# Moving the large SBUF tiles of a three-layer kernel to multiples of 512 bytes

## The reference, cut to what matters

```python
def swiglu(x, w_gate, w_up, w_down):
    return (jax.nn.silu(x @ w_gate) * (x @ w_up)) @ w_down
...
        x = layer_norm(DN_ALPHA * x + y, mix_ln_g[layer], mix_ln_b[layer])
        x = layer_norm(DN_ALPHA * x + swiglu(x, ffn_w_gate[layer], ffn_w_up[layer], ffn_w_down[layer]),
                       ffn_ln_g[layer], ffn_ln_b[layer])
...
    ff = jnp.square(jax.nn.relu(h2 @ w_ff1 + b_ff1)) @ w_ff2 + b_ff2
```

## Time and profile before

| | |
|---|---|
| three runs | 3600.16, 3602.02, 3602.89 us; median 3602.02 us |
| profiled execution, first to last instruction | 3599.7 us |
| around it, against the median | 2.3 us |
| PE busy | 3523.2 us, 98%, 16054 matmuls |
| VectorE, ScalarE, GpSimd busy | 50%, 34%, 15% |
| DMA queue of the loads | 22.5% of 16 engines' span |
| mean granted TensorE clock | 0.987 |

### The profile page before, as it was taken

How to read it: one execution, slowest core, us unless ns; L and a number is a source line. 1 busy time by engine, 2 the same in 40 slices (tenths; PEclk the granted TensorE clock), 3 DMA queues, 4 the chain that set the end, 5 groups by cost and what they waited for, 6 DMA issues and landing times. The chain is left out here.

```text
span 3599.7 us, 41711 instructions
## 1 busy us (share of the span) xinstructions
PE 3523.2 (98%) x16054; PEld 2827.2 (79%) x16054; DVE 1782.8 (50%) x2319; ACT 1234.6 (34%) x1795; POOL 529.2 (15%) x302
## 2 busy tenths in 40 slices
PE   9999999999999999999999999999999899999998
PEld 7768888888887777767888888888877778888886
DVE  7986423233256666667423233564567774323235
ACT  4444410111144444455311112355454442212133
POOL 0007100000042000013100000253223530000004
PEclk9999999999999999999999999999999999999999
DMA  3102213122122111112213123322231222111113
GB/s 105 40 30 89 94 60 109 47 78 86 47 82 82 48 41 47 41 59 77 88 59 105 52 84 108 93 89 94 97 99 48 76 88 88 53 45 48 47 58 100
DMA packets 77474, 259.12 MB, mean 72 GB/s; under 512 B 10288, under 2 KB 11696, under 8 KB 77360
## 3 DMA queue, kind: packets, MB, share of 16 engines
q1 hardware_dynamic: 77360, 257.59, 22.5%
HBM read 244.45 MB, written 4.72 MB: 69 GB/s over the span
## 5 line engine op out<-in xcount | busy, mean ns | idle before, releaser
L202 PE MATMUL ps<-xh,whi 128*128 128x512 f32 x2712 | 941.8, 393 | 14.2 <-POOL xl L494 8.9
L202 PE MATMUL ps<-xh,wlo 128*128 128x512 f32 x2712 | 934.4, 390 | 0.0
L202 PE MATMUL ps<-xl,whi 128*128 128x512 f32 x2712 | 934.1, 390 | 0.0
L185 DVE TENSOR_TENSOR wlo<-stage,whi 128x1024 fp32r<-128x1024 f32 (+1 forms) x361 | 507.2, 1405 | 477.9 <-ACT whi L178 476.7
L178 ACT ACTIVATE whi<-stage 128x1024 fp32r<-128x1024 f32 (+1 forms) x361 | 377.8, 1046 | 1001.2 <-PE ps L202 973.8
L202 PEld LDWEIGHTS ps<-xh,whi 128*128 128x128 f32 x2712 | 511.1, 189 | 130.0 <-POOL xl L494 9.1
L202 PEld LDWEIGHTS ps<-xh,wlo 128*128 128x128 f32 x2712 | 511.2, 188 | 107.3
L202 PEld LDWEIGHTS ps<-xl,whi 128*128 128x128 f32 x2712 | 511.5, 189 | 105.1
L202 PE MATMUL ps<-hh,whi 128*128 128x512 f32 x1216 | 421.5, 395 | 3.1 <-DVE hl L2938 1.6
L202 PE MATMUL ps<-hl,whi 128*128 128x512 f32 x1216 | 420.3, 394 | 0.0
L202 PE MATMUL ps<-hh,wlo 128*128 128x512 f32 x1216 | 420.3, 394 | 0.0
(11 more groups left out here) (453 smaller groups left out, 4013.1 us busy)
## 6 DMA issues: line engine op xcount, KB each, us to landing
stage<-in_w_ff SPq DMA_DIRECT2D x88, 512.0 KB, 3.5
stage<-in_w_gate SPq DMA_DIRECT2D x59, 512.0 KB, 3.4
stage<-in_w_up SPq DMA_DIRECT2D x59, 512.0 KB, 3.4
stage<-in_w_in SPq DMA_DIRECT2D x50, 512.0 KB, 3.4
ada<-in_w_ada SPq DMA_DIRECT2D x48, 512.0 KB, 3.5
stage<-in_w_qkv SPq DMA_DIRECT2D x43, 512.0 KB, 3.4
stage<-in_w_down SPq DMA_DIRECT2D x48, 448.0 KB, 3.3
stage<-in_w_out SPq DMA_DIRECT2D x24, 512.0 KB, 3.4
```

The lines of the kernel that those rows point to most:

```text
L185: dve.tensor_tensor(wlo[slot][:, n], stage[slot][:, n], whi[slot][:, n].bitcast(F32), ALU.subtract).then_inc(w_split, 1)
L202: done = pe.matmul(acc[:, h * HALF:(h + 1) * HALF], wt[slot][:, w], xt[:, b, h * HALF:(h + 1) * HALF], start=b == 0 and wt is whi and xt i ...
```

## The change

It moves tiles, and changes no instruction but for the addresses in it. On all five engines the instructions stand in the same order, with the same shapes and waits.

```diff
+    LINE = 512
+
+    def to_line(name):
+        at = -(-nc.sbuf_base // 32) * 32
+        if at % LINE:
+            sb(name, [P, (LINE - at % LINE) // 4])
+        return nc.sbuf_base
+
+    mod = sb("mod", [P, NMOD, DB])
+    moments = sb("moments", [P, 2, 24])
+    to_line("pad_x")
     x = sb("x", [P, DB, S])
     XH_AT = nc.sbuf_base
     xh = sb("xh", [P, DB, S], F32R)
...
-    mv = sb("mv", [P, 2, 2])
     stats = sb("stats", [P, 2, 2, 6])
-    sd = sb("sd", [P, 2, 1])
-    rstd = sb("rstd", [P, 2, 1])
...
-    mod = sb("mod", [P, NMOD, DB])
     gb2 = sb("gb2", [P, DB])
...
-    moments = sb("moments", [P, 2, 24])
...
-    REGION = -(-nc.sbuf_base // 32) * 32
+    REGION = to_line("pad_region")
```

## The result

| | before | after |
|---|---|---|
| median | 3602.45 us (4 runs, 3600.16 to 3604.06) | 3582.72 us (4 runs, 3581.69 to 3584.48) |
| ratio | | 0.9949, 95% interval 0.9937 to 0.9962 |
| profiled span | 3599.7 us | 3580.5 us |

By the medians the kernel is 19.7 us faster, 0.55%; the ratio, which is not the quotient of the two medians, says 0.51%, and its interval reads as 13.7 to 22.7 us. The forecast was 3578 us, 24.1 us less than before.

The account below looks back on a forecast made before the run. TensorE, busy 98% of the span with a stream of matmuls, was taken as the bound. The profiled 3599.7 us less 24.1 gave 3575.6, plus 2.3 for the median, so 3578 us; range 3485 to 3606 us.

Parts of the forecast that it names:

- the side that had 0.77: Whole kernel: chance of any faster outcome, 0.60 for the region-only forecast plus 0.17 for everything getting faster.
- Matmuls on `hh` go from 233.2 to 226.6 ns: Down projections: with region and fixed tiles at 0, their matmuls reach the up projections' rate of 226.6 ns.
- 3648 matmuls x 6.6 ns: Down projections: 3 x 1216 matmuls at 233.2 - 226.6 ns less each, 24.1 us, all on the path.
- The fixed tiles at 0 bring nothing: Matmuls on `xh`, `xl`: moving fixed tiles from 128 to 0 taken as zero; bounds 96 us gain, 124 us loss.
- The count of 9360: Matmuls affected by moving the fixed tiles, 3 x (2712 + 336 + 72); 6.6 ns more on each would cost 62 us.
- The 260-column rows: Matmuls with moving operands at 16-byte steps: 119 ns each, 10.7 ns extra at every place, cited for zero fixed-tile effect.
- the 32 plain float32 matmuls of rows 8: Matmuls streaming `a_pad`: 430 ns each, giving some 216 ns without the extra and the 96 us bound on fixed-tile gain.
- The tail: Tail of attention's output, `xh` past region weights: 228, then 232 ns, read as pair evidence; gain at most 0.1 us.
- Cover: Other engines' work stays hidden under TensorE by long waits; idle ahead of `hh`'s first matmuls stays 3.1 us.
- Everything faster: Rival, all long products: extra depends on absolute place; 3492 us (0.10) or 3444 us (0.07), chance 0.17.
- Nothing moves: Rival, down projections: the 6.6 ns belong to the SBUF part above byte 142336; 3602 us, chance 0.13.
- Slower: Rival: fixed tiles leave a good absolute place; 3750 us, or 3664 us if only `xh` slows, chance 0.10.

Follow-up runs that it names:

- e4: Changed kernel with fixed tiles and region all at 64 modulo 512 instead of 0; 3579.7 us, ratio 0.9942 to the kernel before.
- e5: Changed kernel with `stage`, `whi`, `wlo` and the region at 64 modulo 512, `x`, `xh`, `xl` at 0; 3631.1 us, ratio 1.0082 to before.
- e1: Changed kernel with fixed tiles kept at 128 modulo 512, so only the region moved to 0; 3599.1 us, ratio 0.9995 to before.
- e10: Changed kernel with fixed tiles at 256 modulo 512, region at 0, some small tiles reordered for room; 3582.1 us, ratio 0.9946 to before.
- the probes: Kernels without the computation, matmuls in a row at many pairs of starts; 60 of 256 columns took 7.44 us at equal starts, 7.25 at (32, 0).
- e8: Probe without the computation: 60 matmuls in a row per pair of starts; float32r, 512 columns: 13.86 us at (0, 0), 14.24 at (32, 0).
- e6: Changed kernel with fixed tiles and region all at 32 modulo 512 instead of 0; 3583.5 us, ratio 0.9949 to before.
- e11: Probe without the computation, with 128, 96, 64 and 32 weight columns; 60 matmuls at equal starts took 13.86, 14.04, 13.99 and 14.06 us.

## Why the prediction was right, and where its sizes were off

The median of 3582.72 us lies in the range (3485 to 3606), 5 us above the forecast, on the side that had 0.77. Of 24.1 us expected, 19.7 came; 24.1 lies 1.4 us outside of the interval.

**Matmuls on `hh` go from 233.2 to 226.6 ns.** Right to the digit: 353 loads in 80 us, as the last part of the prediction asked. Right too was the reading behind it, that the pair counts and not `hh`: e4 leaves `hh` where it was, e5 gives the slow rate to the up projections. Wrong was the size of the line: "half a 128-byte line off" is not the rule; e1 has a difference of a whole 128 bytes and is as slow as before, so moving the region alone to 0 would have brought nothing beyond noise, though it ends on such a line as the fixed tiles do. The period is 256 bytes, and the sign counts. That the chosen places have a difference of 0 is what made the forecast come true; the prediction's rule alone would have allowed e1 too.

**3648 matmuls x 6.6 ns.** The rate was right for the long products (7.43 us found on 1104 matmuls in the last piece of the chain, 7.3 expected). Summed from start to start over the profiled executions, matmuls on `hh` and `hl` take 854.5 us before and 833.2 us after, 21.3 less instead of 24.1; those on `xh` and `xl` at L202 take 2.0 us more (1887.8 and 1889.8), all the rest 0.2 more. That is the 19.2 us of the span. What is missing from the 24.1 are pauses and a lower clock. The unit at 2904.03 took 7.22 us; before it was this row of the chain, from the kernel before:

```profile
2914.73 5.70 PE ps L202 x24
```

1.5 us on 24 matmuls. Windows around it, before and then after, show a mean granted clock of 1.00 and of 0.91; a share of 0.09 of 18 us not granted is 1.6 us:

```profile
2905.00:2922.00 17.00, 15.36 (x78) 12.37 (x77) 10.86 (x16) 5.20 (x7) 7.67 (x5) 1.00 0.30 93
```

```profile
2895.00:2913.00 18.00, 16.57 (x77) 13.67 (x78) 10.33 (x15) 5.20 (x7) 6.96 (x5) 0.91 0.30 88
```

In the 14 us ahead of that unit TensorE had been busy 12.2. Such stretches at the 1.2 GHz level come and go: e10, at the same rates, has 1.00 at the same place and a profiled span of 3577.3 us, 22.4 less than before, and e4 3576.9 us, 22.8 less. So 22 to 23 us came in these two executions, in which that unit runs at the full clock. That this fall of the clock follows from the change was not shown; the median of the runs is what counts, and it has 20.

**The fixed tiles at 0 bring nothing.** Right: xh's rate was 226.0 to 226.6 ns at 0, 32, 64, 128 and 256. The rows that were to bound it were weaker than they looked. The count of 9360 was too large for a loss of 6.6 ns each, as e5 shows: the 1224 of the attention lost 2.5. The 260-column rows say nothing of 512 columns: with 256 columns the probes settle at 113.3 to 120.0 ns, and equal starts are the slowest; the mean of 119 ns over many starts hid that. And the 32 plain float32 matmuls of rows 8 are records, of which e8 has two to a matmul (120 for 60), so the 216 ns taken from them is half a record and no matmul's cost.

**The tail.** Here the evidence was misread. With both operands at 0, PE in order of time of the kernel after, against the earlier trace rows:

```profile
1635.87 0.40 PE L2010 MATMUL ps<-xh,tail_wlo 128*128 128x512 f32 x1
...
1637.92 0.39 PE L2010 MATMUL ps<-xh,tail_wlo 128*128 128x512 f32 x1
...
1639.11 0.39 PE L2010 MATMUL ps<-xl,tail_whi 128*128 128x512 f32 x1
...
1641.43 0.39 PE L2010 MATMUL ps<-xh,tail_wlo 128*128 128x512 f32 x1
```

Nine in 2.05 us, 228 ns, and after the pause ten in 2.32 us, 232 ns: as before. So the 232 ns that the prediction took for the mark of a bad pair stand at equal starts too, in this short run after a pause. It supported a true statement by chance; "settles at 227 ns" did not come.

**Cover.** Right in the main: the engines behind TensorE kept their long waits. But the idle time ahead of `hh` was to stay at 3.1 us, and the prediction named its growth as a sign of being wrong; it is 4.0 us, 0.7 of the 0.9 more in waits for `wlo` (1.2 before, 1.9 after). This and the unit at the lower clock make up most of the 2.8 us that `hh` and `hl` fell short.

**The rivals.** *Everything faster* falls: no pair of starts tried settles under 226.7 ns at 512 columns, so at least 13.3 ns beyond the columns stay. *Nothing moves* falls with e4: same part of SBUF, fast. *Slower* falls with e4, e6 and e10, which put the fixed tiles at three more places without loss; but e5 shows a loss of its kind, from a pair and not from a place: 64 bytes between `xl` and `stage` cost 29 us. The Trainium skill's sentence that TensorE never waits on anyone (SBUF — State Buffer, "Who interferes with whom") cannot be carried over to TensorE's own two streams: with the same instructions at other starts a matmul takes 226.7 or 233.3 ns (whether one stream then waits for the other is not shown). The Trainium skill's gap of N / 2.4 GHz + 2.5 ns for an isolated warm matmul (TensorE: Matmul & The Clock Gate, "Back-to-back issue gap") is right for bfloat16 in e8, 13.13 us less 0.39 over 59 = 216 ns, and is 11 ns short for float32r.

**Open.** What the 13.3 ns are, why a pair's starts matter with a period of 256 bytes, and why the order of starts turns round at 256 columns. The 13.3 ns are the same at 256, 384 and 512 columns, and e11 excludes that they shrink with the weight load. No version here beats the changed kernel beyond its interval; e4, e6 and e10 equal it.

## What to carry to other kernels

In a kernel that streams float32r matmuls of 512 columns past 128x128 weights, list the starts of moving and stationary tiles modulo 256 bytes and make them equal (multiples of 32) for every pair that runs long; a few unnoticed bytes of small tiles between two large ones cost 3% of each such matmul. Equal was enough at every multiple of 32 tried, no particular line is needed, and the check is cheap: divide a window inside a long product by its weight loads, product by product, and ask why two of one shape differ. Short runs (6 matmuls gained 1.5 ns each), other widths and fewer weight columns have rates and an order of their own: they are no evidence for this rule, and a kernel made of them needs a map of its own.

## What the runs showed of the hardware that was not expected

- The time of a 128x512 float32r matmul depends on the two starts: 226.7 ns at differences of 0 and 256 bytes (starts that are multiples of 32), 229 at +64 and +320 (from a stationary start of 0), 230 to 237 at the others, 233.3 at most of them, 239 where both start at 4 bytes.
- With 256 columns the best place found is +192, 7.06 us for 60, and equal starts take 7.44: 5% the other way.
- Bfloat16 (216 ns) and plain float32 (430 ns a record) showed no dependence on the starts tried (moving at 0 and 64, bfloat16 at 32 too, stationary at 0).
- With 32 weight columns the dependence is nearly gone (14.01 to 14.07 us for 60), and every pair is slower than the best with 128 columns (13.86 us). With 96 and 64 weight columns equal starts are not the best pair.
